# Two of the 24 modulation groups computed on TensorE between w_o and w_gate instead of on VectorE

## The chip, the cores and the metric

The kernel runs on one core of one Trainium2 chip. The metric is the device time of one execution in microseconds. Weights come from HBM by DMA, in chunks of one megabyte.

## What is computed

Two blocks in a row work on x, 256 positions by 2048 values, all in fp32. The first is a transformer block that is modulated by a second input c:

```python
mod = jax.nn.silu(c) @ w_ada[l] + b_ada[l]            # w_ada: 2048 x 12288
shift_a, scale_a, gate_a, shift_f, scale_f, gate_f = jnp.split(mod, ADA_CHUNKS, axis=-1)
h = rms_norm(x, g_attn_pre[l]) * (1.0 + scale_a[:, None]) + shift_a[:, None]
proj = h @ w_in[l]                                    # 2048 x 5456
...                                                   # two kinds of attention
mixed = jnp.concatenate([diff_out, dsa_out], axis=-1) @ w_o[l]
x = x + gate_a[:, None] * rms_norm(mixed, g_attn_post[l])
h = rms_norm(x, g_ffn_pre[l]) * (1.0 + scale_f[:, None]) + shift_f[:, None]
ff = (jax.nn.silu(h @ w_gate[l]) * (h @ w_up[l])) @ w_down[l]
x = x + gate_f[:, None] * rms_norm(ff, g_ffn_post[l])
```

The second block (latent attention, a convolution branch and their projections) uses no modulation and is not touched.

w_ada has 12288 columns, that is 24 groups of 512. Groups 0 to 3 are shift_a, 4 to 7 scale_a, 8 to 11 gate_a, 12 to 15 shift_f, 16 to 19 scale_f, 20 to 23 gate_f. Group 15 is the last quarter of shift_f, group 19 the last quarter of scale_f. Since x has 2048 columns, four groups of 512 make up one vector, and the fourth group serves the fourth quarter of the operand h alone.

## The kernel before

**Chunks and their ring.** `PLAN` (from `chunk_plan`, line 54) lists all 476 chunks of the program in one order. A chunk has 512 rows of a weight by up to 512 columns. SyncE loads them in that order into five buffers (`raw`, `NRAW` = 5): chunk c may be loaded when chunk c - 5 has been used (`load_chunk` in `sync_program`, the DMA at line 2440).

**A linear chunk** is two units. For each unit ScalarE copies 256 rows into a high half (`whi`, line 1033), VectorE subtracts it for the low half (`wlo`, line 1643), and TensorE makes three products out of them (lines 566 to 568, 12 matmuls of 512 columns a unit). `Walk.chunk` puts the splits of a unit into the queues of ScalarE and VectorE two units ahead (`AHEAD` = 2) of the place where its products stand:

```python
self.split_to(UNIT_AT[LIN[min(self.unit + AHEAD, len(LIN) - 1)]])
```

So while the last two units of w_o are worked off, the two units of the first w_gate chunk are split, and only then does the program go on to what follows w_o.

**A w_ada chunk** is used in one of two ways. Groups 8 to 23 are summed on VectorE (`ada_step`, line 1626: four passes a chunk of acc += raw * column, the first group of a row at line 1623, and one last sum at line 1635). Then TensorE turns the sum into columns of modT or into a row (`ada_take`, lines 501, 502 and 506), which runs as a side job in lane 1, and VectorE adds the bias (`mod`, line 1607). Groups 0 to 7 (`ADA_ON_PE`) are products of TensorE (`ada_products`, line 520): four matmuls a chunk with a stationary operand `cs32` of 32 columns, of which one holds silu(c) and 31 are zero. ScalarE copies the result out (`gather`), TensorE makes columns of it (`ada_columns`, line 531). These groups are needed first and are all done in the first quarter of w_in.

**What sets the order.** Every engine runs the same walk over the plan and emits its own part. Side jobs (attention in lanes 0 and 1, `soon` jobs in lane 2) advance one step per unit (`tick`). VectorE's w_ada chunks are dealt between the linear chunks by `more` in `chunk_plan`: 26 of them between the 24 later chunks of w_in (`W_IN_SHARE`), the remaining 16 between those of w_o (`W_O_SHARE` = 15), one after each chunk but the last.

**Between w_o and w_gate** stands a chain. For each output group `post_group` has ScalarE square it (line 1295) and VectorE multiply it by the gate (line 2073, `P<-bank,G` in the trace). After the last one VectorE makes the root's input (1688), ScalarE the root (1065), VectorE adds to x (1695, eight parts), ScalarE squares x (1302), VectorE makes `gs` (2110) and `diag` (1717), and TensorE turns the first quarter of x with it (`turn_quarter(0)`, line 582). Then follow shift and scale on VectorE (1744) and the high and low halves of the operand (1110, 1734), and w_gate begins.

## Time and profile before

| | |
|---|---|
| time, median of 3 runs | 2428.31 us (2427.94 to 2430.77) |
| the profiled execution | 2428.22 us, span 2426.9 us |
| TensorE matmuls busy | 2291.2 us, 94% |
| VectorE busy | 1399.5 us, 58% |
| ScalarE busy | 1062.3 us, 44% |
| mean DMA rate | 208 GB/s |

In the 40 slices of 60.7 us, TensorE is at nine tenths or more from the tenth slice on; before that it falls to seven and eight tenths in places. VectorE has 9 and 8 tenths in the fourth and fifth slice, then six, and four to five from the eleventh on. A share over the whole span says little here: the stages differ, and a saving counts only where TensorE waits.

### The profile page before, as it was taken

Reading aid. Unit: us, or ns where it says so; the run is one execution under the profiler, and the core shown is the slowest. Engines: PE = TensorE matmul, PEld = TensorE weight load, DVE = VectorE, ACT = ScalarE, POOL = GpSimd, SP = SyncE. Lnnn points to the kernel's source line nnn. Section 1 sums busy time; section 2 is a strip of 40 time slices with the busy share of each in tenths; the row PEclk is TensorE's granted clock in tenths of the full one; section 3 lists DMA queues with packets and bytes.
Section 4 is the critical chain, followed back from the end, with each engine's and each line's share of the span. In section 5 each row is a group of like instructions: output and inputs, shape, how many; then the busy total and the mean of one; then the engine's idle time right before and its main releaser. Section 6 shows DMA issues by size and latency. Waiting matters only on the chain.

```text
span 2426.9 us, 26309 instructions
## 1 busy us (share of the span) xinstructions
PE 2291.2 (94%) x10768; PEld 1861.1 (77%) x10768; DVE 1399.5 (58%) x1903; ACT 1062.3 (44%) x1469; POOL 0.7 (0%) x5
## 2 busy tenths in 40 slices
PE   4898989798999999999999999999999999999998
PEld 2676667676878888888887878788888888888886
DVE  1459898686666464454555555454544554554554
ACT  2333534444434444444444555555444444444443
POOL 0000000000000000000000000000000000000000
PEclk7999999899999999999999999999999999999999
DMA  7888678484776575556554644444555556556553
GB/s 296 333 314 306 216 262 285 153 306 166 247 273 243 192 259 191 191 191 191 191 189 143 210 157 154 153 152 152 185 196 192 188 184 197 183 186 194 187 190 139
DMA packets 255455, 505.69 MB, mean 208 GB/s; under 512 B 9077, under 2 KB 19662, under 8 KB 254182
## 3 DMA queue, kind: packets, MB, share of 16 engines
q1 hardware_dynamic: 255334, 504.00, 61.6%
q8 instruction: 85, 1.39, 0.2%
q14 instruction: 36, 0.29, 0.0%
HBM read 499.77 MB, written 4.19 MB: 208 GB/s over the span
## 4 chain that ended last, share of the span: by engine, by line
PE 82%; DVE 10%; ACT 3%; DMA 3%; issue 2%; SPq 0%; DVEq 0%; ACTq 0%
PE bank L566 26%; PE bank L568 25%; PE bank L567 25%; DVE wlo L1643 3%; DVE acc L1626 2%; PE bank L582 2%; DMA raw<-in_w_in_dram 2%; ACT whi L1033 1%; PE bank L650 1%; DMA raw<-in_w_ada_dram 1%; PE bank L520 1%; PE bank L590 1%; DVE x L1695 0%; ACT Ex_b L1162 0%; PE bank L673 0%
## 5 line engine op out<-in xcount | busy, mean ns | idle before, releaser
L1643 DVE TENSOR_TENSOR wlo<-raw,whi 128x1024 fp32r<-128x1024 f32 (+2 forms) x760 | 910.5, 1205 | 887.6 <-ACT whi L1033 887.1
L1033 ACT ACTIVATE whi<-raw 128x1024 fp32r<-128x1024 f32 (+2 forms) x760 | 790.1, 1044 | 1035.2 <-PE bank L568 949.1
L566 PE MATMUL bank<-whi,Ahi 128*128 128x512 f32 (+2 forms) x2304 | 912.5, 396 | 37.8 <-DVE wlo L1643 21.2
L567 PE MATMUL bank<-wlo,Ahi 128*128 128x512 f32 (+2 forms) x2304 | 897.0, 389 | 0.0
L568 PE MATMUL bank<-whi,Alo 128*128 128x512 f32 (+2 forms) x2304 | 896.6, 389 | 0.0
L566 PEld LDWEIGHTS bank<-whi,Ahi 128*128 128x128 f32 x2304 | 438.1, 190 | 141.1 <-DVE wlo L1643 31.3
L568 PEld LDWEIGHTS bank<-whi,Alo 128*128 128x128 f32 x2304 | 437.7, 190 | 90.3
L567 PEld LDWEIGHTS bank<-wlo,Ahi 128*128 128x128 f32 x2304 | 438.5, 190 | 83.2
L1626 DVE SCALAR_TENSOR_TENSOR acc<-raw,cs,acc 128x512 f32<-128x512 f32 x224 | 153.4, 746 | 0.0
L566 PE MATMUL bank<-whi,Fhi 128*128 128x512 f32 x352 | 137.7, 391 | 0.0
L568 PE MATMUL bank<-whi,Flo 128*128 128x512 f32 x352 | 137.0, 389 | 0.0
L567 PE MATMUL bank<-wlo,Fhi 128*128 128x512 f32 x352 | 137.0, 389 | 0.0
L566 PE MATMUL bank<-whi,Bhi 128*128 128x512 f32 x256 | 101.0, 395 | 0.0
L568 PE MATMUL bank<-whi,Blo 128*128 128x512 f32 x256 | 99.8, 390 | 0.0
L567 PE MATMUL bank<-wlo,Bhi 128*128 128x512 f32 x256 | 99.7, 390 | 0.0
L566 PEld LDWEIGHTS bank<-whi,Fhi 128*128 128x128 f32 x352 | 66.1, 188 | 14.3 <-issue 0.8
L568 PEld LDWEIGHTS bank<-whi,Flo 128*128 128x128 f32 x352 | 66.1, 188 | 14.0
L567 PEld LDWEIGHTS bank<-wlo,Fhi 128*128 128x128 f32 x352 | 66.1, 188 | 13.4
L520 PE MATMUL bank<-raw,cs 128*32 128x512 f32 x256 | 35.9, 681 | 21.3 <-DMA raw<-in_w_ada_dram 21.3
L568 PEld LDWEIGHTS bank<-whi,Blo 128*128 128x128 f32 x256 | 48.1, 188 | 10.2
L566 PEld LDWEIGHTS bank<-whi,Bhi 128*128 128x128 f32 x256 | 48.1, 188 | 9.9 <-issue 0.3
L567 PEld LDWEIGHTS bank<-wlo,Bhi 128*128 128x128 f32 x256 | 48.1, 188 | 9.6
(291 smaller groups left out, 1345.2 us busy)
## 6 DMA issues: line engine op xcount, KB each, us to landing
raw<-in_w_in_dram SPq DMA_DIRECT2D x156, 1024.0 KB, 5.0
raw<-in_w_ada_dram SPq DMA_DIRECT2D x96, 1024.0 KB, 5.3
raw<-in_w_gate_dram SPq DMA_DIRECT2D x44, 1024.0 KB, 5.1
raw<-in_w_up_dram SPq DMA_DIRECT2D x44, 1024.0 KB, 5.1
raw<-in_w_down_dram SPq DMA_DIRECT2D x44, 1024.0 KB, 5.0
raw<-in_w_o_dram SPq DMA_DIRECT2D x16, 1024.0 KB, 5.2
raw<-in_w_o_mla_dram SPq DMA_DIRECT2D x16, 1024.0 KB, 4.9
raw<-in_w_o_conv_dram SPq DMA_DIRECT2D x16, 1024.0 KB, 4.9
```

Of the source, the lines that this page charges most:

```text
L520: ins = pe.matmul(m.bank[b][32 * jj:32 * jj + 32, :], m.cs32[:, 4 * j + jj, :], m.raw[:, c % NRAW, jj, :], start=(j == 0), stop=(j == 3))
L566: pe.matmul(o, a_hi, w_hi, start=beg, stop=False)
L567: pe.matmul(o, a_hi, w_lo, start=False, stop=False)
L568: ins = pe.matmul(o, a_lo, w_hi, start=False, stop=fin)
L582: ins = pe.matmul(o, i, m.diag[:, tb, :], start=True, stop=True) if scaled else pe.transpose(o, i, m.ident)
L590: ins = pe.transpose(m.bank[b][:, tb * P:tb * P + P], src(tb), m.ident)
L650: pe.matmul(m.bank[ln.bank[mm]][:, PART[tb]], l, r, start=(i == 0), stop=False, skip_group_check=True)
L1033: act.activation(m.whi[:, i % NHL, :, 0:n], m.raw[:, c % NRAW, 2 * h:2 * h + 2, 0:n], ACT.Copy).then_inc(m.s_hi, 1)
L1626: ins = dve.scalar_tensor_tensor(out=o, in0=w, scalar=col, in1=o, op0=ALU.mult, op1=ALU.add)
L1643: dve.tensor_tensor(m.wlo[:, i % NHL, :, 0:n], m.raw[:, c % NRAW, 2 * h:2 * h + 2, 0:n], m.whi[:, i % NHL, :, 0:n].bitcast(F32), ALU.subtr ...
```

## The change

Groups 15 and 19 leave VectorE. Their eight chunks are taken out of the deal between w_in and w_o and stand in the plan after the last w_o chunk, numbers 132 to 139, right ahead of w_gate's first chunk, which is number 140 in both kernels. TensorE makes the products of all eight right behind the last w_o product, into banks 6 and 7. The gathering copies, the columns, the bias and the last quarter of the gains `gs` become side jobs inside the first w_gate linear. The stationary operand for them is a new tile `cs_gap`, filled by VectorE during w_o. The side jobs of the other groups use bank 4 instead of bank 6 from late in w_o on (`idle_bank`). VectorE's other chunks are dealt anew: 22 in w_in, 12 in w_o, none between the last four w_o chunks. A load that reuses the buffer of one of the new chunks waits for that chunk's product (`prod_at`).

```diff
-W_IN_SHARE = 26
-W_O_SHARE = 15
+W_IN_SHARE = 22
+W_O_SHARE = 12
-ADA_ON_PE = (4, 0, 5, 1, 6, 2, 7, 3)
+ADA_ON_PE = (4, 0, 5, 1, 6, 2, 7, 3, 15, 19)
...
-    rest = [("ada", g, j) for g in ADA_ON_PE for j in range(4)]
-    rest += [("ada", g, j) for g in range(8, 20) for j in range(4)]
+    rest = [("ada", g, j) for g in ADA_ON_PE[:8] for j in range(4)]
+    rest += [("ada", g, j) for g in range(8, 20) if g not in ADA_ON_PE for j in range(4)]
...
     assert not rest
+    plan += [("ada", g, j) for g in ADA_ON_PE[8:] for j in range(4)]
     rest = [("ada", g, j) for g in range(20, 24) for j in range(4)]
...
+        self.idle_bank = 6
...
+        self.cs_gap = sb("cs_gap", [P, KD, 32])
...
             _, g, j = PLAN[c]
-            b = 6 + ADA_ON_PE.index(g) % 2
+            idx = ADA_ON_PE.index(g)
+            b = 6 + idx % 2
+            need.wait_ge(m.s_cs, 1 if idx < 8 else 2)
+            cs = m.cs32 if idx < 8 else m.cs_gap
...
-                ins = pe.matmul(m.bank[b][32 * jj:32 * jj + 32, :], m.cs32[:, 4 * j + jj, :], m.raw[:, c % NRAW, jj, :],
+                ins = pe.matmul(m.bank[b][32 * jj:32 * jj + 32, :], cs[:, 4 * j + jj, :], m.raw[:, c % NRAW, jj, :],
                                 start=(j == 0), stop=(j == 3))
             ins.then_inc(m.s_prod if j < 3 else m.filled[b], 1)
+            m.prod_at[c] = (m.s_prod, 3 * idx + j + 1) if j < 3 else (m.filled[b], k.uses[b])
...
     mix_operand(12, (4, 5))
+    k.idle_bank = 4
...
+    def gap_columns():
+        ada_columns(8)
+        ada_columns(9)
+
+    def gate_side(j):
+
+        if j < 3:
+            k.soon(turn_quarter, 4 * j + 4)
+        if j == 0:
+            k.soon(gap_columns)
...
             linear("w_gate", 512 * cg, 512, m.A_op, shifted(8),
-                   before=lambda j: k.soon(turn_quarter, 4 * j + 4) if cg == 0 and j < 3 else None)
+                   before=gate_side if cg == 0 else None)
...
+    def gap_gather():
+        gather(4)
+        k.use(6), k.use(7)
...
     linear("w_o", 512, 512, ks=(4,), s=sets[1])
+    need.wait_ge(*rt_at[0])
+    v.up(dve.memset(m.cs_gap[:, :, :], 0.0))
+    settle()
+    dve.tensor_copy(m.cs_gap[:, :, 0], m.cs[:, :]).then_inc(m.s_cs, 1)
...
-    released(*(mod_at[g] for g in range(12, 20)))
-    v.up(dve.scalar_tensor_tensor(out=m.gs[:, :], in0=m.modT[:, 64:80], scalar=1.0, in1=m.cols[:, R_G2:R_G2 + 16],
-                                  op0=ALU.add, op1=ALU.mult))
+    def gains(q, n):
+
+        released(*(mod_at[g + i] for g in (12, 16) for i in range(q, q + n)))
+        ks = slice(4 * q, 4 * q + 4 * n)
+        v.up(dve.scalar_tensor_tensor(out=m.gs[:, ks], in0=m.modT[:, 64 + 4 * q:64 + 4 * q + 4 * n], scalar=1.0,
+                                      in1=m.cols[:, R_G2 + 4 * q:R_G2 + 4 * q + 4 * n], op0=ALU.add, op1=ALU.mult))
+
+    gains(0, 3)
...
+    def gap_mods():
+        for idx in (8, 9):
+            b = 6 + idx % 2
+            k.use(b)
+            mod(ADA_ON_PE[idx], b, k.use(b))
+        gains(3, 1)
+        settle()
...
-                idx, j = ADA_ON_PE.index(before[1]), before[2]
-                if j < 3:
-                    need.wait_ge(m.s_prod, 3 * idx + j + 1)
-                else:
-                    need.wait_ge(m.filled[6 + idx % 2], 2 * (idx // 2) + 1)
+                need.wait_ge(*m.prod_at[c - NRAW])
```

VectorE at the end of w_o in the kernel before. `P_76<-bank,G` is the first row of the chain between w_o and w_gate; the last two `wlo` rows ahead of it are the two units of w_gate's first chunk.

```order
L1626 SCALAR_TENSOR_TENSOR acc<-raw,cs,acc 128x512 [waits s_v] x2
L1635 TENSOR_TENSOR acc<-acc 128x512 [waits s_ada,s_v]
L1643 TENSOR_TENSOR wlo<-raw,whi 128x1024 [waits s_hi] x2
L1607 TENSOR_TENSOR modT<-bank,bT 128x4 [waits s_filled6]
L1643 TENSOR_TENSOR wlo<-raw,whi 128x1024 [waits s_hi] x2
L2073 TENSOR_TENSOR P_76<-bank,G 128x512 [waits s_psq] x2
L1688 TENSOR_REDUCE rstd<-ssq 128x2
```

The same place in the changed kernel (its line numbers are 30 or so higher).

```order
L1638 TENSOR_TENSOR modT<-bank,bT 128x4 [waits s_filled4]
L2104 TENSOR_TENSOR P_76<-bank,G 128x512 [waits s_psq] x2
L1674 TENSOR_TENSOR wlo<-raw,whi 128x1024 [waits s_hi] x8
L2104 TENSOR_TENSOR P_76<-bank,G 128x512 [waits s_psq] x2
L1719 TENSOR_REDUCE rstd<-ssq 128x2
```

VectorE's w_ada steps are gone from the last four w_o chunks; the two units of w_gate's first chunk still stand ahead of `P_76<-bank,G`.

SyncE's loads from the end of w_o to w_gate before:

```order
L2440 DMA raw<-in_w_ada_dram 128x4x512 [waits s_lo]
L2440 DMA raw<-in_w_o_dram 128x4x512 [waits s_ada]
L2440 DMA raw<-in_w_gate_dram 128x4x512 [waits s_lo]
L2440 DMA raw<-in_w_gate_dram 128x4x512 [waits s_ada]
L2440 DMA raw<-in_w_gate_dram 128x4x512 [waits s_lo]
L2440 DMA raw<-in_w_gate_dram 128x4x512 [waits s_ada]
L2440 DMA raw<-in_w_up_dram 128x4x512 [waits s_lo] x4
```

and in the changed kernel, where `s_prod` and `s_filled6` are raised by TensorE's products of the new chunks:

```order
L2491 DMA raw<-in_w_o_dram 128x4x512 [waits s_lo]
L2491 DMA raw<-in_w_ada_dram 128x4x512 [waits s_ada]
L2491 DMA raw<-in_w_ada_dram 128x4x512 [waits s_lo] x4
L2491 DMA raw<-in_w_ada_dram 128x4x512 [waits s_prod] x3
L2491 DMA raw<-in_w_gate_dram 128x4x512 [waits s_filled6]
L2491 DMA raw<-in_w_gate_dram 128x4x512 [waits s_prod] x3
L2491 DMA raw<-in_w_up_dram 128x4x512 [waits s_filled7]
```

The last three w_ada loads and the first four of w_gate wait for products of TensorE.

VectorE late in w_in, where the trace has a long run of w_ada steps, before:

```order
L1626 SCALAR_TENSOR_TENSOR acc<-raw,cs,acc 128x512 [waits s_v] x2
L1643 TENSOR_TENSOR wlo<-raw,whi 128x1024 [waits s_hi] x2
L1626 SCALAR_TENSOR_TENSOR acc<-raw,cs,acc 128x512 [waits s_v,s_raw1]
L1626 SCALAR_TENSOR_TENSOR acc<-raw,cs,acc 128x512 [waits s_ada]
L1626 SCALAR_TENSOR_TENSOR acc<-raw,cs,acc 128x512 [waits s_v] x2
L1626 SCALAR_TENSOR_TENSOR acc<-raw,cs,acc 128x512 [waits s_v,s_raw2]
L1626 SCALAR_TENSOR_TENSOR acc<-raw,cs,acc 128x512 [waits s_ada]
L1626 SCALAR_TENSOR_TENSOR acc<-raw,cs,acc 128x512 [waits s_v] x2
L1635 TENSOR_TENSOR acc<-acc 128x512 [waits s_ada,s_v]
L1643 TENSOR_TENSOR wlo<-raw,whi 128x1024 [waits s_hi]
L1607 TENSOR_TENSOR modT<-bank,bT 128x4 [waits s_filled6]
L1643 TENSOR_TENSOR wlo<-raw,whi 128x1024 [waits s_hi]
```

and now:

```order
L2061 SCALAR_TENSOR_TENSOR Ex_b<-Ex_b,sm_b 128x256 [waits s_v]
L1674 TENSOR_TENSOR wlo<-raw,whi 128x1024 [waits s_hi]
L1657 SCALAR_TENSOR_TENSOR acc<-raw,cs,acc 128x512 [waits s_raw3]
L1657 SCALAR_TENSOR_TENSOR acc<-raw,cs,acc 128x512 [waits s_ada]
L1657 SCALAR_TENSOR_TENSOR acc<-raw,cs,acc 128x512 [waits s_v] x2
L1666 TENSOR_TENSOR acc<-acc 128x512 [waits s_ada,s_v]
L1674 TENSOR_TENSOR wlo<-raw,whi 128x1024 [waits s_hi] x2
L1712 SCALAR_TENSOR_TENSOR Alo<-bank,gsub,Ahi 128x512 [waits s_oph,s_gsub]
```

One chunk's steps less stand ahead of the low halves there.

## Rows read from the trace of the kernel before

**Rows 1.** The page: busy time, share of the span and instructions of each engine.

```profile
PE 2291.2 (94%) x10768; PEld 1861.1 (77%) x10768; DVE 1399.5 (58%) x1903; ACT 1062.3 (44%) x1469; POOL 0.7 (0%) x5
```

**Rows 2.** Windows: busy time by engine, granted clock, DMA; the first row names the columns.

```profile
core 0: us, PE busy (x) PEld busy (x) DVE busy (x) ACT busy (x) POOL busy (x), PEclk, DMA share, GB/s
...
240.00:432.00 192.00, 166.76 (x829) 129.53 (x828) 167.85 (x335) 89.78 (x202) 0.00 (x0) 0.95 0.71 246
432.00:560.00 128.00, 111.16 (x533) 90.48 (x531) 97.15 (x154) 51.95 (x99) 0.00 (x0) 0.93 0.72 254
...
600.00:1200.00 600.00, 598.39 (x2652) 490.38 (x2651) 332.03 (x330) 249.61 (x260) 0.00 (x0) 1.00 0.65 218
```

**Rows 3.** Waits of TensorE, 280 to 560 us: total, times, longest.

```profile
PE bank L663 <- DVE Ex_b L2030: 16.6, 4, 8.8
...
PE bank L566 <- DVE wlo L1643: 3.7, 3, 2.8
```

**Rows 4.** The chain that ended last, 552 to 576 us: start, duration, what.

```profile
552.74 0.79 PE bank L506 x8
...
559.88 1.29 DVE P L2073 x2
...
569.43 3.78 PE bank L582 x16
...
574.04 0.47 PE bank L566
```

**Rows 5.** Timelines of TensorE, VectorE and ScalarE at the end of w_o.

```profile
558.73 0.39 PE L568 MATMUL bank<-whi,Alo 128*128 128x512 f32 x1
...
550.93 2.35 DVE L1643 TENSOR_TENSOR wlo<-raw,whi 128x1024 fp32r<-128x1024 f32 x2
...
557.53 1.23 DVE L1643 TENSOR_TENSOR wlo<-raw,whi 128x1024 fp32r<-128x1024 f32 x1 [2.38 <-ACT whi L1033]
...
559.15 0.60 ACT L1295 ACTIVATE P<-bank 128x512 f32<-128x512 f32 x1 [1.66 <-PE bank L568]
```

**Rows 6.** DMA issues, median us to landing last: 559 to 600, then 500 to 560.

```profile
raw<-in_w_up_dram SPq DMA_DIRECT2D x3, 1024.0 KB, 5.1
...
raw<-in_w_o_dram SPq DMA_DIRECT2D x7, 1024.0 KB, 7.1
```

**Rows 7.** Timeline of TensorE at the kernel's start, and a window there.

```profile
25.27 1.07 PE L520 MATMUL bank<-raw,cs 128*32 128x512 f32 x8 [0.95 <-DMA raw<-in_w_ada_dram]
34.78 1.93 PE L520 MATMUL bank<-raw,cs 128*32 128x512 f32 x8 [8.44 <-DMA raw<-in_w_ada_dram]
...
39.89 1.55 PE L520 MATMUL bank<-raw,cs 128*32 128x512 f32 x8 [0.62 <-DMA raw<-in_w_ada_dram]
...
34.78:42.00 7.22, 5.98 (x29) 1.23 (x30) 0.00 (x0) 0.32 (x1) 0.00 (x0) 0.57 1.06 406
```

**Rows 8.** Timelines in the first w_gate linear, ScalarE and TensorE.

```profile
581.84 1.99 ACT L1033 ACTIVATE whi<-raw 128x1024 fp32r<-128x1024 f32 x2
...
581.40 0.39 PE L566 MATMUL bank<-whi,Ahi 128*128 128x512 f32 x1
```

**Rows 9.** Timelines: three waits of TensorE, and VectorE ahead of two of them.

```profile
418.33 1.22 PE L650 MATMUL bank<-qT_b 64*128 64x256 f32 x4 [4.47 <-DVE modT L1607]
437.21 0.47 PE L663 MATMUL bank<-const,Ex_b 128*128 128x128 f32 x1 [2.78 <-DVE Ex_b L2030]
489.57 0.46 PE L673 MATMUL bank<-P,ET_a 128*128 128x128 f32 x2 [1.94 <-DVE ET_a L1912]
...
410.89 5.39 DVE L1626 SCALAR_TENSOR_TENSOR acc<-raw,cs,acc 128x512 f32<-128x512 f32 x8
...
428.77 4.07 DVE L1626 SCALAR_TENSOR_TENSOR acc<-raw,cs,acc 128x512 f32<-128x512 f32 x6
```

**Rows 10.** Two groups of TensorE instructions with first and last start, 600 on.

```profile
L501 PE MATMUL bank<-acc,const x8: 592/594/596, 667.9 to 897.0; 128*128 128x512 f32 x8
...
L582 PE MATMUL bank<-const,gt x8: 270/272/299, 674.5 to 678.0; 128*128 128x128 f32 x8
```

More of the change, by code:

```diff
@@ L382, in __init__ @@
         self.A_op = self.Ahi, self.Alo
+        self.prod_at = {}
         base = shelf.top
@@ L534, in idle @@
     def idle():
-        ada_take(k.take(), 6)
+        ada_take(k.take(), k.idle_bank)
         yield
@@ L629, in first_part @@
         return linear("w_in", *win_cols(cg), m.A_op, shifted(0), ks=(4 * q,))
-    need.wait_ge(m.s_cs, 1)
     ada_products(0)
@@ L1036, in idle @@
         k.take()
-        k.use(6)
+        k.use(k.idle_bank)
         yield
@@ L1321, in scalar_program @@
     mix_operand(12, (4, 5))
+    k.idle_bank = 4
     linear("w_o", 512, 512, ks=(4,), s=sets[1])
@@ L1344, in scalar_program, with gate_side @@
     F_at = [None]
+    def gap_gather():
+        gather(4)
+        k.use(6), k.use(7)
+    def gate_side(j):
+        if j < 3:
+            k.soon(shifted, m.tmpB, j + 1)
+        if j == 0:
+            k.soon(gap_gather)
     def ff_turn(kf):
@@ L1357, in scalar_program @@
         for cg in range(*third):
-            s = linear("w_gate", 512 * cg, 512,
-                       before=lambda j: k.soon(shifted, m.tmpB, j + 1) if cg == 0 and j < 3 else None)
+            s = linear("w_gate", 512 * cg, 512, before=gate_side if cg == 0 else None)
             k.finish_side()
@@ L1646, in idle @@
     def idle():
-        mod(k.groups[k.take()], 6, k.use(6))
+        mod(k.groups[k.take()], k.idle_bank, k.use(k.idle_bank))
         yield
@@ L2092, in vector_program @@
     mix_operand(12, (4, 5))
+    k.idle_bank = 4
     linear("w_o", 512, 512, ks=(4,), s=sets[1])
+    need.wait_ge(*rt_at[0])
+    v.up(dve.memset(m.cs_gap[:, :, :], 0.0))
+    settle()
+    dve.tensor_copy(m.cs_gap[:, :, 0], m.cs[:, :]).then_inc(m.s_cs, 1)
     y_at = []
@@ L2128, in ff_turn, with gate_side @@
         lo_pair(m.F_op, 4 * kf + 2, 5, [None])
+    def gap_mods():
[5 more added lines that the diff above has]
+        settle()
+    def gate_side(j):
+        if j < 3:
+            k.soon(ffn_operand, j + 1)
+        if j == 1:
+            k.soon(gap_mods)
     ffn_operand(0)
@@ L2133, in vector_program @@
         for cg in range(*third):
-            s = linear("w_gate", 512 * cg, 512,
-                       before=lambda j: k.soon(ffn_operand, j + 1) if cg == 0 and j < 3 else None)
+            s = linear("w_gate", 512 * cg, 512, before=gate_side if cg == 0 else None)
             gate_at = set_at(s)
@@ L2499, in build @@
         m = Machine(nc, A, out, ctx)
-        sync_program(m)
         tensor_program(m)
@@ L2504, in build @@
         gpsimd_program(m)
+        sync_program(m)
 def constants():
```

## The prediction

> **What bounds the kernel now.** I read the page first: TensorE is busy for 2291.2 of 2426.9 us [rows 1]. The windows by stage say where it is not [rows 2]. From 600 us on it is full (598.39 of 600), so nothing done for VectorE helps there. In 240 to 432 it is busy 166.76 of 192 us and VectorE 167.85; in 432 to 560, 111.16 of 128 and VectorE 97.15. These two stretches hold the attention steps, w_in and w_o, and VectorE's sums of w_ada, four passes a chunk. The view of waits names what TensorE lacked in 280 to 560, 40 us in all [rows 3]; the largest part, 16.6, belongs to one step of the attention chains (Ex_b), and only 3.7 to a weight half that came late (wlo). Then the chain through the pause [rows 4]: the last w_o product ends at 558.73 + 0.39 = 559.12 us, called E below. ScalarE and VectorE take the last group out of its banks (the latter from 559.88 on), norm it, square it, and at 569.43 TensorE turns x with diag; w_gate starts at 574.04. The pause is a chain of ScalarE and VectorE; TensorE stands idle for 10.3 us of it.
>
> **What stands just ahead of that chain** decides the case. VectorE runs its rows in order, and the low halves of the first w_gate chunk are split two units ahead: the second of the two is the row at 557.53, before the row at 559.88 [rows 4, 5]. The order shows the same in the changed kernel: of the eight wlo rows ahead of P, the last two are the halves of chunk 140, the first of w_gate. Before, that chunk had been in memory for long. Now eight w_ada chunks (132 to 139) are loaded ahead of it, through five buffers, and four of these loads, 137 to 140, may only be issued when TensorE's products of chunks 132 to 135 are done. Those stand in TensorE's queue behind the last w_o product. So chunk 140 is asked for after E, as the fourth of four loads, and the chain of the pause waits behind its splits.
>
> **The pause, step by step from E.** Chunks 132 to 136 are there at E: the last of them follows the split of the last w_o chunk, some 6 us before E (the pair of splits at 550.93 ended at 553.28, rows 5), and a lone megabyte lands in 5.1 us [rows 6]. A chunk's products took 1.07 us at best and 1.93 us at a granted clock of 0.57, the level of 1.2 GHz [rows 7]; after a stage at the full clock I take 1.07. So load 137 is issued at E + 1.2 and lands at E + 1.2 + 5.1 = 6.3. The next three were asked for by then (one product each 1.07 us) and follow at the rate of a full queue: in the start of the kernel the products of three chunks in a row begin from 34.78 to 39.89, 2.56 us apart, at 406 GB/s [rows 7]. Chunk 140 is there at 6.3 + 3 x 2.56 = E + 14.0. Its two splits take 1.06 us on ScalarE and then 2.35 us on VectorE (as the pair at 550.93, rows 5): E + 17.5. Only then comes the row that before began at E + 0.76. **The chain moves by 16.8 us**, and all that hangs on it. Bounds: 15 us if load 137 leaves right at E (5.1 + 7.7 + 1.06 + 2.35 - 0.76 = 15.5, and half a microsecond less for what I may have wrong in the handoffs), 19 us if loads land in 7.1 us as they do at 500 to 560 [rows 6]. Product 139 ends at about E + 11.5 + 1.9 = 13.4; that is cover, since the chain reaches diag only at 10.3 + 16.8 = E + 27.1. TensorE is idle before that turn again for over 10 us, so the turn's 3.78 us [rows 4] stay as they are. The loads of 141 to 144 finish inside the longer pause, so w_gate lacks nothing.
>
> The Trainium skill ("DMA: Bandwidth & Descriptors", section "Where 436 GB/s comes from") says that loads from HBM are held by the memory at about 358 GB/s a core. This trace shows 406 [rows 7]. By the page, 1.05 MB would take 2.93 us instead of 2.56 and the chain would move by 1.1 us more; the sum goes by the rows.
>
> **Added in w_gate.** ScalarE copies the products of groups 15 and 19 out (two copies), TensorE sums them into columns (eight small matmuls), VectorE adds the bias twice and makes the last four gains. The order puts the copies behind the first whi of the row at 581.84, and TensorE's columns ahead of its third unit, which began at 581.40 [rows 8]. That whi ends at 582.9, two copies of 0.6 (such a read of a bank took 0.60, rows 5) make 584.0; TensorE waits until then and needs 0.8 for the second group's columns (0.79, rows 4), 2.5 + 0.8. **+3.3 us**; bounds 1.6 (only the columns, twice 0.79) and 4.5 (a copy more of waiting). Groups 20 to 23 now use bank 4, which the turns of gt use too: TensorE's first row for such a group, at 667.9, lies 6.6 us ahead of the next turn, at 674.5, which waits for gt then anyway [rows 10], so I cost it at nothing; without that cover it would be one wait of about 1 us, four times.
>
> **Removed.** VectorE loses eight chunks of 2.7 us (eight passes took 5.39), 21.6 us, and two short sums at their ends that I leave out [rows 9]; TensorE loses twice 0.79 us of columns [rows 4]. What reaches the path is what TensorE waited for behind such a chunk: 4.47 us at 418.33, where VectorE had two chunks in a row (5.39), 2.78 at 437.21 after six passes (4.07), 1.94 at 489.57 after one chunk more, and 0.9 in the two short ones of the three waits for wlo (3.7 - 2.8): 10.1 us [rows 3, 9]. The order takes a chunk away before the first three; I take 8 of the 10.1. The other waits for Ex_b, 16.6 - 2.8 with one of 8.8 among them [rows 3], stand mostly behind the search for the top keys, where as many chunks stay. Against it: a side job more or less shifts lane b, and its last scores (qT_b) come one unit later, so that the last chain of attention has one unit (2.7 us, twelve products) less beside it; part of that is bought back since ScalarE's two softmaxes no longer meet. I charge 1.0. **-8.6 us** (8.0 + 1.6 - 1.0). Bounds: -23.2, if every microsecond of VectorE counted (21.6 + 1.6), and +3, if the shift costs a whole unit and nothing is won.
>
> The memset and copy of cs_gap on VectorE (under 1 us) fall where it loses a chunk; nothing.
>
> **Sum:** 16.8 + 3.3 - 8.6 = +11.5 us. The profiled run took 2428.22 us, 1.3 more than its span, and the median is 2428.31; so 2439.8 us.
>
> **Rivals.**
> *All of the relief counts.* VectorE is 87% busy in 240 to 432; if it sets the pace there from end to end, and the waits for Ex_b shrink too, the whole 23.2 us come off: 16.8 + 3.3 - 23.2 = -3.1, 2425 us, not slower. It decides from a relief of 20.1 us on. For it: that share, about TensorE's own. Against: TensorE's idle time there is what its named waits give, and those behind a chunk sum to 10.1 only.
> *The pause isn't held.* Should the splits of chunk 140 not stand ahead of the norm after all, the pause would grow only until product 139 is done, E + 13.4 against 10.3: 3.1 + 3.3 - 8.6 = -2.2, 2426 us. The order speaks against it.
> *The relief is eaten.* One unit less beside the last attention chain and new phases elsewhere: 16.8 + 3.3 + 3 = +23.1, 2451 us. For it: most of the 40 us are latencies between engines which no lighter queue shortens.
> *A slower stream.* If the loads land as they did under load at the end of w_o, 7.1 us after their issue instead of 5.1 [rows 6], chunk 140 comes 2 us later and the sum is 13.5: 2442 us.
>
> **How the numbers follow.** Forecast 0.60, all of the relief 0.10, not held 0.06, relief eaten 0.14, slower stream 0.10. A measurement tells 0.2% apart, 4.9 us: faster means under 2423.4, slower over 2433.2. Slower takes the forecast (all but a tail of relief above 15 us), the third and fourth rivals: 0.81. Faster, 0.05, is the far half of the first rival. The rest, 0.14, is the same. The range runs from 2430 to 2451: relief up to 18 us below, the third rival above.
>
> **What would show it.** VectorE's row P after the last w_o product: right if it starts 15 to 19 us after E (before 0.76) with the two wlo rows just ahead of it and "ACT whi" or the DMA of w_gate as what they waited for; wrong if it starts within 2 us. TensorE idle before the first turn in two pieces, between products for the DMA of w_ada, and some 13 us for diag. The first w_gate product about 31.7 us after E (before, at 574.04, 14.9). TensorE's waits at about 418 and 437 gone, and E itself 6 to 10 us earlier than 559.1; if E is later, the relief was eaten; if it is 20 us earlier, the first rival holds. A wait of 2 to 3 us before the columns in w_gate. Windows from 600 us on unchanged in length. The forecast is wrong above all if ScalarE or VectorE gets to the norm before w_gate's first chunk.

## The result and the profile after

| | before | changed |
|---|---|---|
| median of 4 runs | 2428.12 us (2427.86 to 2430.77) | 2451.52 us (2451.44 to 2452.88) |
| ratio | 1 | 1.0096, 95% interval 1.0084 to 1.0109 |
| span of the profiled execution | 2426.9 us | 2451.5 us |

The change costs 23.4 us. The forecast was 11.5 us, and the result lies half a microsecond beyond the end of the forecast's range. The page of the changed kernel, beside [rows 1], has TensorE 17 us busier and VectorE 21 us less busy:

```profile
PE 2308.1 (94%) x10832; PEld 1866.4 (76%) x10832; DVE 1378.8 (56%) x1872; ACT 1062.1 (43%) x1471; POOL 0.7 (0%) x5
```

Windows of the changed kernel, with the columns of [rows 2]:

```profile
240.00:557.00 317.00, 276.40 (x1339) 218.53 (x1339) 241.29 (x450) 135.33 (x285) 0.00 (x0) 0.94 0.66 226
557.00:588.00 31.00, 13.20 (x81) 5.22 (x80) 11.45 (x22) 9.73 (x25) 0.00 (x0) 0.63 0.80 304
588.00:604.00 16.00, 13.77 (x65) 11.40 (x66) 8.88 (x13) 5.70 (x8) 0.00 (x0) 0.82 0.16 45
640.00:1200.00 560.00, 558.09 (x2467) 456.77 (x2466) 312.58 (x314) 230.53 (x240) 0.00 (x0) 1.00 0.65 218
```

The pause is now 31 us, and the start of w_gate runs at a granted clock of 0.82. From 640 us on TensorE is as full as before; a loss of 2 us near 697, told below, is too small to show in so long a window. Four marks of TensorE's timeline split both spans without a remainder: E, the end of the last w_o product (559.12 us before, as in the prediction); the first w_gate product; the turn of the fourth quarter of x (the last thing particular to that linear); the end.

| us | before | changed | difference | forecast |
|---|---|---|---|---|
| E | 559.12 | 557.06 | -2.1 | -8.6 |
| E to the first w_gate product | 14.92 | 31.35 | +16.4 | +16.8 |
| first w_gate product to the fourth turn | 17.32 | 24.68 | +7.4 | +3.3 |
| fourth turn to the end | 1835.5 | 1838.4 | +2.9 | 0 |
| sum | | | +24.6 | +11.5 |

**The pause** went as forecast. The chain that ended last, in the changed kernel (start, duration, what; it answers to [rows 4]):

```profile
557.05 3.62 PE bank L529 x32
560.69 10.19 DMA raw<-in_w_gate_dram
570.89 1.07 ACT whi L1054
571.98 2.36 DVE wlo L1674 x2
574.35 1.20 DVE P L2104 x2
...
583.82 3.78 PE bank L592 x16
```

TensorE works off the products of the chunks that are there, the load of w_gate's first chunk lands at 570.89, E + 13.8, and only behind its splits comes VectorE's P row, 17.3 us behind E. TensorE's own rows in this stretch show the stream and the idle time ahead of the turn:

```profile
565.76 1.94 PE L529 MATMUL bank<-raw,cs_gap 128*32 128x512 f32 x8 [1.49 <-DMA raw<-in_w_ada_dram]
568.31 1.94 PE L529 MATMUL bank<-raw,cs_gap 128*32 128x512 f32 x8 [0.62 <-DMA raw<-in_w_ada_dram]
583.82 3.78 PE L592 MATMUL bank<-diag,x 128*128 128x128 f32 x16 [13.57 <-DVE diag L1748]
```

Loads whose products start 2.55 us apart are again more than 400 GB/s (the window of 561 to 571 gives 409), so the memory limit of 358 GB/s that the Trainium skill states ("DMA: Bandwidth & Descriptors", "Where 436 GB/s comes from") did not bind here.

**The relief** (the -8.6 us that were to come off ahead of E) did not come. Waits of TensorE in the changed kernel, 280 to 557 us (total, times, longest), beside [rows 3]:

```profile
PE bank L672 <- DVE Ex_b L2061: 12.0, 3, 7.3
PE bank L682 <- DVE ET_a L1943: 7.6, 3, 5.1
PE bank L576 <- DVE P L2076: 6.9, 1, 6.9
PE bank L576 <- DVE Alo L1710: 4.0, 1, 4.0
...
PE bank L659 <- DVE modT L1638: 0.6, 1, 0.6
```

In the kernel before, the same view had these for the same causes:

```profile
PE bank L663 <- DVE Ex_b L2030: 16.6, 4, 8.8
PE bank L566 <- DVE P L2045: 6.5, 1, 6.5
PE bank L650 <- DVE modT L1607: 4.5, 1, 4.5
...
PE bank L673 <- DVE ET_a L1912: 3.1, 3, 1.9
PE bank L566 <- DVE Alo L1679: 1.5, 1, 1.5
```

The waits that the forecast named are gone or short: 3.9 of 4.5 us for modT, the 2.8 for Ex_b at 437 (1.0 is left, for ScalarE), the 1.9 for ET_a at 489 [rows 9]. But a wait of 5.1 us for ET_a stands where 0.7 stood, the one for Alo is 2.5 us longer, and smaller ones are new. All waits of this view add up to 40.3 us now and to 39.9 before: VectorE has eight chunks less, and TensorE waits as long as it did. The 2.1 us by which E is earlier are about the size of what TensorE itself lost there, the columns of two groups (twice 0.79 us). VectorE's timeline ahead of the ET_a copy, changed kernel, with the row of TensorE that waited for it, shows why. TensorE began its transposes for that copy at 367.9 and has nothing left to do from 371.5 on:

```profile
369.64 2.73 DVE L1657 SCALAR_TENSOR_TENSOR acc<-raw,cs,acc 128x512 f32<-128x512 f32 x4
372.29 1.22 DVE L1674 TENSOR_TENSOR wlo<-raw,whi 128x1024 fp32r<-128x1024 f32 x1
...
374.35 0.29 DVE L1889 TENSOR_TENSOR P<-rt 128x128 f32<-128x128 f32 x1
...
374.76 1.22 DVE L1674 TENSOR_TENSOR wlo<-raw,whi 128x1024 fp32r<-128x1024 f32 x1
375.90 0.55 DVE L1943 COPY ET_a<-bank 128x384 f32<-128x384 f32 x1
...
376.59 0.77 PE L682 MATMUL bank<-P,ET_a 128*128 128x128 f32 x2 [5.14 <-DVE ET_a L1943]
```

and in the kernel before, where the transposes began at 369.5 and TensorE was busy until 374.0:

```profile
369.59 0.88 DVE L1623 TENSOR_SCALAR acc<-raw,cs 128x512 f32<-128x512 f32 x2
370.38 1.41 DVE L1626 SCALAR_TENSOR_TENSOR acc<-raw,cs,acc 128x512 f32<-128x512 f32 x2
371.71 2.35 DVE L1643 TENSOR_TENSOR wlo<-raw,whi 128x1024 fp32r<-128x1024 f32 x2
373.98 0.55 DVE L1912 COPY ET_a<-bank 128x384 f32<-128x384 f32 x1
...
374.68 0.46 PE L673 MATMUL bank<-P,ET_a 128*128 128x128 f32 x2 [0.68 <-DVE ET_a L1912]
```

A chunk stands ahead of the copy in both. Now six rows of the other lane's rotation (rt and P, 1.3 us) stand there too, so that the copy comes 1.9 us later, and TensorE is through with its own work 2.5 us earlier: together the 4.5 us by which the wait has grown. Dealing the chunks anew moved the lanes against each other.

**The first w_gate linear** has two stretches at the lower clock, 1.2 instead of 2.4 GHz (0.63 us a product instead of 0.39). Timeline of TensorE, changed kernel:

```profile
588.41 0.77 PE L576 MATMUL bank<-whi,Ahi 128*128 128x512 f32 x1 [0.81 <-issue]
...
591.53 0.63 PE L577 MATMUL bank<-wlo,Ahi 128*128 128x512 f32 x1
...
592.35 0.40 PE L576 MATMUL bank<-whi,Ahi 128*128 128x512 f32 x1
...
599.59 1.95 PE L541 MATMUL bank<-const,acc 128*128 128x1 f32 x16 [1.82 <-ACT acc L1076]
...
602.72 0.63 PE L578 MATMUL bank<-whi,Alo 128*128 128x512 f32 x1
...
605.70 2.07 PE L592 MATMUL bank<-diag,x 128*128 128x128 f32 x16
```

From the first product to the second turn it took 4.65 us, 2.84 before: +1.8. From there to the third turn 12.64 us against 7.24: 1.8 for the wait, 1.8 for the columns, 1.8 for the second stretch at 1.2 GHz. Of the last term of the table, 1.6 us are one more such stretch, after a wait of 1.91 us for gt at 697.06 (from there to the next turn of gt 4.8 us, against 3.2). Before, the wait was 1.61 us long [rows 10, at 674.5] and had full clock behind it. A wait of 0.5 us for a low half at 620.97 is new too; the last 0.5 us have no row of their own.

### The profile page after: what moved, and what is told of

Its sections match the earlier page's. It is cut to its first block, busy times and chain, and to the rows that moved or that the text cites. A ratio compares the mean times of both kernels' runs of the same rounds, so it can differ in the third digit from the quotient of the medians.

```text
span 2451.5 us, 26398 instructions
## 1 busy us (share of the span) xinstructions
PE 2308.1 (94%) x10832; PEld 1866.4 (76%) x10832; DVE 1378.8 (56%) x1872; ACT 1062.1 (43%) x1471; POOL 0.7 (0%) x5
## 4 chain that ended last, share of the span: by engine, by line
PE 82%; DVE 10%; ACT 4%; DMA 3%; issue 2%; SPq 0%; DVEq 0%; ACTq 0%
PE bank L576 25%; PE bank L578 25%; PE bank L577 25%; DVE wlo L1674 3%; DVE acc L1657 2%; DMA raw<-in_w_in_dram 2%; PE bank L592 2%; ACT whi L1054 1%; PE bank L659 1%; PE bank L529 1%; DMA raw<-in_w_ada_dram 1%; PE bank L600 0%; DVE x L1726 0%; DMA raw<-in_w_gate_dram 0%; ACT Ex_b L1183 0%
## 5 line engine op out<-in xcount | busy, mean ns | idle before, releaser
L1657 DVE SCALAR_TENSOR_TENSOR acc<-raw,cs,acc 128x512 f32<-128x512 f32 x196 | 134.4, 745 | 0.1
L578 PEld LDWEIGHTS bank<-whi,Blo 128*128 128x128 f32 x256 | 48.1, 188 | 10.3
```

Source lines behind the costliest of these rows:

```text
L578: ins = pe.matmul(o, a_lo, w_hi, start=False, stop=fin)
L1657: ins = dve.scalar_tensor_tensor(out=o, in0=w, scalar=col, in1=o, op0=ALU.mult, op1=ALU.add)
```

## The experiments

Theory: the pause is held by the splits of w_gate's first chunk; the relief was lost to where the deal puts VectorE's chunks among the lanes; the first linear lost twice to the clock. Each time below is a median, each ratio is to the kernel before on the same chip, with its interval. The marks are those of the table above; they come from the one execution of each kernel that was profiled, which can lie some microseconds beside its median. How far E moves by itself can be read off the six kernels that share the deal of 22 + 12 (changed, e1, e2, e3, e4, e8): it lies between 555.4 and 560.6.

| kernel | us | ratio | E | to w_gate | to 4th turn | rest |
|---|---|---|---|---|---|---|
| changed | 2451.5 | 1.0096 (1.0084 to 1.0109) | 557.1 | 31.4 | 24.7 | 1838.4 |
| e1, w_gate's chunk first | 2440.4 | 1.0044 (1.0027 to 1.0061) | 560.6 | 19.8 | 22.9 | 1837.5 |
| e2, columns later | 2446.8 | 1.0074 (1.0059 to 1.0089) | 557.0 | 31.3 | 21.0 | 1835.8 |
| e3, groups left out, 22 + 12 | 2430.3 | 1.0005 (0.9995 to 1.0014) | 556.0 | 14.9 | 19.0 | 1837.2 |
| e6, left out, 26 + 8 | 2422.7 | one execution | 549.8 | 14.9 | 19.6 | 1837.1 |
| e7, left out, 18 + 16 | 2417.8 | one execution | 545.0 | 15.1 | 19.4 | 1837.1 |
| e4, 26 idle products | 2453.1 | 1.0101 (1.0086 to 1.0116) | 558.0 | 34.4 | 22.9 | 1839.8 |
| e8, 14 idle products | 2450.4 | 1.0096 (1.0081 to 1.0112) | 555.4 | 30.2 | 22.8 | 1837.5 |
| e5, one group, 24 + 14 | 2430.9 | 1.0013 (1.0003 to 1.0022) | 551.4 | 16.8 | 25.9 | 1838.7 |
| e9, changed, 18 + 16 | 2447.8 | 1.0077 (1.0064 to 1.0091) | 551.1 | 31.3 | 24.9 | 1836.1 |
| e13, changed, 26 + 8 | 2441.0 | 1.0056 (1.0042 to 1.0069) | 550.3 | 31.4 | 24.5 | 1838.1 |
| e10, three mends, 18 + 16 | 2424.6 | 0.9985 (0.9976 to 0.9993) | 546.6 | 17.9 | 19.2 | 1837.0 |
| e16, three mends, 16 + 18 | 2429.9 | 1.0010 (1.0001 to 1.0019) | 554.6 | 18.6 | 19.2 | 1836.2 |
| e11, one group mended, 22 + 16 | 2440.9 | 1.0051 (1.0037 to 1.0065) | 562.4 | 19.5 | 20.2 | 1839.1 |
| before | 2428.1 | 1 | 559.1 | 14.9 | 17.3 | 1835.5 |
| e15, before, 24 + 18 | 2433.7 | 1.0033 (1.0021 to 1.0044) | 561.1 | 14.9 | 17.3 | 1835.6 |
| e12, before, 22 + 20 | 2442.8 | 1.0054 (1.0040 to 1.0067) | 568.5 | 14.9 | 17.3 | 1835.6 |
| e14, before, 30 + 12 | 2437.4 | 1.0035 (1.0022 to 1.0049) | 564.1 | 14.9 | 19.0 | 1837.5 |

### The pause: w_gate's first chunk loaded ahead of the eight

```diff
-    plan += [("ada", g, j) for g in ADA_ON_PE[8:] for j in range(4)]
+    gap = [("ada", g, j) for g in ADA_ON_PE[8:] for j in range(4)]
...
                     lin(w, 4 * q, 512 * cg, 512)
+                    plan += gap
+                    gap = []
...
     k.take_rest()
+    ada_products(PLAN.index(("ada", ADA_ON_PE[8], 0)))
     need.wait_ge(m.s_diag, 4)
```

> The changed kernel with one thing moved: the first chunk of w_gate is loaded before the eight chunks of groups 15 and 19, and TensorE still takes their products in the pause. Theory (the splits of that chunk, queued ahead of the norm's work on ScalarE and VectorE, hold the pause): the P row comes at E+1 instead of E+17.3 and the diagonals at E+10; but the eighth product, its load the fifth behind the last w_o product, ends about E+13.7, later than the diagonals, so that the first product of w_gate comes at E+18.5 instead of E+31.4. About 13 us less than the changed kernel, 2438.5. Rival 1 (the products themselves, or the loads' share of the memory, lengthen the pause): the first product of w_gate stays beyond E+28 and the time above 2448. Rival 2 (the second chunk of w_gate, now the last of the nine loads, is late instead): PE stalls inside the first linear for about 5 us and the time is about 2443.

Measured: the ratio falls by 0.52 points, some 12.6 us, and the way from E to w_gate from 31.4 to 19.8. VectorE's rows at the end of w_o, with P now 0.75 us behind E (560.62) as before the change:

```profile
559.03 1.23 DVE L1677 TENSOR_TENSOR wlo<-raw,whi 128x1024 fp32r<-128x1024 f32 x1 [1.44 <-ACT whi L1057]
561.37 1.29 DVE L2107 TENSOR_TENSOR P<-bank,G 128x512 f32<-128x512 f32 x2 [1.12 <-ACT P L1319]
```

and TensorE's:

```profile
575.82 3.30 PE L594 MATMUL bank<-diag,x 128*128 128x128 f32 x16
```

The splits were what held the pause; the products are not dear in themselves. What stays, 4.9 us, is the eighth load: the turn can start only behind its product, 15.2 us behind E, 1.5 later than I expected. E itself is 3.5 us later than in the changed kernel, with the same waits within 1 us each; the granted clock was 0.89 instead of 0.94 in 430 to 460 us and 0.79 instead of 0.87 in 460 to 500.

### The pause with one group

```diff
-ADA_ON_PE = (4, 0, 5, 1, 6, 2, 7, 3, 15, 19)
+ADA_ON_PE = (4, 0, 5, 1, 6, 2, 7, 3, 15)
...
         ada_columns(8)
-        ada_columns(9)
```

ScalarE's copy and VectorE's bias for group 19 go too, and the shares are 24 and 14.

> The changed kernel with group 15 alone on TensorE in the pause; group 19 is VectorE's again (24 of its chunks with w_in, 14 with w_o). Four chunks stand in the pause instead of eight, so that the first chunk of w_gate is the fifth load behind them and has landed when w_o ends. Theory (the pause is lengthened only by splits that wait for a late load): the P row comes at E+1, the diagonals at E+10, the first product of w_gate at E+15 as in the kernel before, where E is the end of the last w_o product; one column group instead of two takes 1 us less in the first linear. E near 558, in all 2434 to 2436. Rival (the products of chunks in the pause themselves cost, in proportion to their number): the first product of w_gate at E+23, the time about 2443.

Measured: 16.8 us from E to w_gate, and 1.0013. With four chunks in place of eight, w_gate's chunk is the fifth load, and the hold is nearly gone; P came 2.6 us behind E instead of 0.8, since its load landed only at 550.65. The rival, a cost in proportion to the products, is out: it had w_gate at E + 23. The time was better than I expected because E came at 551.4. The first linear took 25.9 us, not the 1 us less than in the changed kernel that I expected of a single column group: its two stretches at 1.2 GHz were 5.0 and 5.5 us long, against 4.1 and 3.2.

### The columns one chunk later

```diff
-        if j == 0:
+        if j == 1:
             k.soon(gap_columns)
```

> The changed kernel with TensorE's two column groups of 15 and 19 one chunk of w_gate later in its own order (behind the third quarter's turn instead of the second's); ScalarE and VectorE are as they were. Theory (TensorE reached them before ScalarE had gathered them, waited 1.82 us, and the half clock of 602.6 to 605.7 follows that wait and those small products): the wait goes, and the half-clock stretch with it, 3 to 3.5 us less, about 2448.3. Rival (the half clock comes from the small products alone, since 16 products of one column keep the engine little occupied): only the wait of 1.8 us goes and half clock comes after the columns all the same, about 2449.7. Rival 2 (VectorE now waits for the columns and the third operand is late): no gain, 2451.5 or more.

Measured: the first linear 21.0 instead of 24.7 us, the ratio 0.22 points lower (5.3 us, more than the 3 to 3.5 expected). The profiled span is 6.3 us shorter, but 2.6 of them lie behind the fourth turn, where the stretch at 1.2 GHz near gt did not come. TensorE:

```profile
600.25 1.95 PE L592 MATMUL bank<-diag,x 128*128 128x128 f32 x16
604.77 1.84 PE L541 MATMUL bank<-const,acc 128*128 128x1 f32 x16
609.33 1.95 PE L592 MATMUL bank<-diag,x 128*128 128x128 f32 x16
```

No wait, and full clock behind the columns (9.08 us from turn to turn, 7.24 + 1.84). The small products alone do not bring the half clock; in the changed kernel, and in e1, e4, e5, e8, e9 and e13 too, it followed the wait of 1.8 to 1.9 us with them behind it (in e13 the columns themselves already ran at it, 3.36 us instead of 1.95).

### Products of constants in the pause

```diff
     k.take_rest()
+    for r in range(26):
+        pe.matmul(m.bank[5][:, 0:384], m.ident, m.const[:, 0:384], start=True, stop=True)
     need.wait_ge(m.s_diag, 4)
```

> The changed kernel with 26 products of constants (384 columns, into a bank that nobody reads then) added on TensorE behind the eight chunks' products, in the idle 13.6 us of the pause; nothing else changes. Theory (the first products of w_gate ran at half the clock from 588.4 to 592.0 because the engine had been idle for 13.6 us, and the turn ahead of them too, 3.78 instead of 1.95): turn 1.8 us shorter, the first linear's start 1.8 us shorter, 3 to 3.6 us less, about 2448.2. Rival (the half clock there has another cause, such as the column groups' small products in the pause): no gain from the added products, 2451.5. Rival 2: they run at half clock throughout and end after the diagonals, which costs up to 3 us, 2454.

> The changed kernel with 14 products of constants in the pause instead of 26 (26 took 17.8 us at 0.68 us each, kept the full clock, but ended 4 us after the diagonals). Theory (the idle pause costs the clock): they end before the diagonals, the turn takes 1.95 us instead of 3.78 and the first quarter of w_gate's products 2.85 us instead of 4.65; 3 to 3.6 us less than the changed kernel, about 2448. Rival (what is won is given back later by a stretch at half clock elsewhere): the first quarter is shorter but the time stays within 1 us of 2451.5.

Measured: 26 ended 4 us too late (rival 2), but the turn took 1.95 us and the way to the second turn 2.85. With 14 they ended in time:

```profile
581.89 2.05 PE L592 MATMUL bank<-diag,x 128*128 128x128 f32 x16 [3.43 <-DVE diag L1747]
585.58 0.47 PE L576 MATMUL bank<-whi,Ahi 128*128 128x512 f32 x1 [1.63 <-issue]
588.42 1.95 PE L592 MATMUL bank<-diag,x 128*128 128x128 f32 x16
```

So the half clock at the start comes from the idle pause: 1.1 us less up to w_gate and 1.8 less in it. Yet the median is no better than that of the change by more than its uncertainty (1.0096 both times, to within 3 us for the change and 4 us for e8). The trace has the gain of 3 us, the timing neither shows nor excludes it.

### The relief: the groups left out, and three deals

```diff
-    plan += [("ada", g, j) for g in ADA_ON_PE[8:] for j in range(4)]
...
-            k.soon(gap_columns)
...
-            k.soon(gap_gather)
...
+    for g in (15, 19):
+        v.up(dve.memset(m.modT[:, 4 * g:4 * g + 4], 0.0))
...
-            mod(ADA_ON_PE[idx], b, k.use(b))
...
```

The products, copies and columns of groups 15 and 19 are left out, and their columns of modT are zeros, so that a quarter of the second operand is computed from other values. In the two further deals `W_IN_SHARE` and `W_O_SHARE` are 26 and 8, and 18 and 16; the second number is the count of w_o steps over which the rest is spread. With 16 steps a chunk stands behind each w_o chunk, the last one too; with 15, as before the change and in e9, e10 and e16, the last w_o chunk has none behind it.

> The changed kernel with groups 15 and 19 left out altogether (their loads, products, gather and columns; the eight columns of the modulation are zeros, so a quarter of the second operand is computed from other values). What stays of the change is the new deal of VectorE's chunks. Theory (from the trace of the changed kernel, whose last w_o product ends 2.1 us earlier than before): the last w_o product ends near 557, the pause is 14.9 us long, the first linear of w_gate runs as before, so about 2426.2 to 2426.5, at most 0.1% faster than the kernel before. Rival (the relief is the 8 us that the waits of before promised, and the loads of the eight chunks in the changed kernel ate it): the last product ends near 551 and the time is about 2420.

> As the run without groups 15 and 19 (their eight columns of the modulation are zeros), but the chunks of VectorE dealt 26 to w_in, as before the change, and 8 to w_o, instead of 22 and 12. Theory (the relief of 8 us of waits came, and the new deal of w_in's chunks made new waits of 5.1 us for ET_a and 2.5 us more for Alo by the places where a chunk stands ahead of a lane's copy): with the old deal in w_in the wait of 5.1 us for ET_a at about 376 is gone, the 4.5 us for modT at about 418 is back, and the waits of the w_o stretch shrink; the last w_o product ends at 552 to 556, instead of 556 to 557. Rival (the waits come with any deal of 34 chunks, being the lanes' own chains): the ET_a wait stays at 5 us and the end does not move by more than 1 us.

> As the run without groups 15 and 19, but dealt 18 to w_in and 16 to w_o (w_o as before the change, w_in relieved of all eight). Theory: the wait of 5.1 us for ET_a at 376 changes by over 1 us, since other operations now stand ahead of that copy, and the waits of the w_o stretch stay as in the kernel before (2.8, 1.9 and 0.9 us); the last product of w_o ends at 554 to 558. Rival (the lanes' own chains set the waits): within 1 us of the run dealt 22 and 12 both at 376 and at the end.

Measured: E at 556.0, 549.8 and 545.0 for the same 34 chunks, the last two from the only execution of their kernel. The pause is 14.9 again in the first two and 15.1 in the third. E came as forecast in e3, yet its median is no faster than the kernel before (2430.3, expected 2426.2 to 2426.5): 1.6 us went into a stretch at 1.2 GHz at the start of w_gate, 1.7 came behind the fourth turn, and the other executions were mostly longer than the profiled one. TensorE's wait for ET_a, in the runs with 26 and with 18 in w_in:

```profile
373.45 0.46 PE L681 MATMUL bank<-P,ET_a 128*128 128x128 f32 x2 [0.65 <-DVE ET_a L1938]
```

```profile
368.54 0.46 PE L681 MATMUL bank<-P,ET_a 128*128 128x128 f32 x2 [2.10 <-DVE ET_a L1938]
```

It is 5.15 us with 22. The rival (the lanes' own chains set these waits) falls. Both came earlier than I expected (552 to 556 with 26, 554 to 558 with 18). The 5 us between the two are no more than E moved under a single deal; that both are ahead of 22 is clear of it. With 26 the wait for modT at 417 is there again (4.45 us), with 18 it is not.

### Does the relief add to the whole change?

```diff
-W_IN_SHARE = 22
-W_O_SHARE = 12
+W_IN_SHARE = 18
+W_O_SHARE = 15
```

and 26 and 8 in the other run.

> The changed kernel, whole, with one number pair changed: VectorE's chunks dealt 18 to w_in and 16 to w_o (the latter as in the kernel before) instead of 22 and 12. Theory (the change lost most of its relief to the places of its deal): the last w_o product ends near 546 instead of 557, the pause and the first linear are as in the changed kernel, so that the time falls by 10 to 11 us to about 2441. Rival (the relief cannot be had together with the loads of the eight chunks, which were left out of the runs that showed it): the end stays near 557 and the time at 2450.

> The changed kernel, whole, dealt 26 to w_in (as before) and 8 to w_o. Theory (22 is a bad number, 26 is not, and the relief adds to the rest): the last w_o product ends near 550 instead of 557, as in the run without the groups, the pause is 31.3 us, the first linear 24.7; about 2445, 6 to 7 us less than the change. Rival (with the eight loads behind w_o only a part of the relief is left, since dealing 18 gave 4 us of 10): 2448 or more.

Measured: with 26, E at 550.3 and 10 us off the time, more than the 6 to 7 expected. With 18, E at 551.1 instead of 546 and only 4 to 5 us off. The order of TensorE's work up to E is that of e10 below, whose E was 546.6, and their waits agree but for one that is 1 us shorter in e9. What differs is the clock. Windows of 370 to 430 and 430 to 460 us, first e9, then e10 (the column ahead of the DMA share):

```profile
370.00:430.00 60.00, 54.72 (x267) 43.40 (x267) 47.04 (x89) 27.02 (x63) 0.00 (x0) 0.91 0.74 258
430.00:460.00 30.00, 26.06 (x152) 21.35 (x152) 19.77 (x41) 13.27 (x39) 0.00 (x0) 0.94 0.53 177
```

```profile
370.00:430.00 60.00, 52.85 (x273) 41.82 (x272) 48.09 (x90) 28.82 (x66) 0.00 (x0) 0.97 0.73 252
430.00:460.00 30.00, 23.07 (x141) 19.05 (x141) 18.46 (x42) 15.42 (x48) 0.00 (x0) 0.99 0.49 172
```

0.06 of 60 us and 0.05 of 30 are 5.1 us of full clock, against 4.5 us at E. By this estimate the clock accounts for the profiled execution; why the other executions of e9 were no faster, and what lowered the clock, is left open.

### Would another deal alone have done it?

```diff
-W_IN_SHARE = 26
+W_IN_SHARE = 22
```

and 24 in a second run, both on the kernel before; 30, with `W_O_SHARE` = 12, in a third.

> The kernel before with nothing changed but the deal of its 42 chunks: 22 with w_in and 20 with w_o instead of 26 and 16. Theory (the waits of the attention stage hang on where chunks stand among the lanes' jobs, so that the same work dealt otherwise gives another time): the end of w_o moves by over 2 us one way or the other, the times lie outside 2426 to 2430. Rival (only the number of VectorE's chunks counts): within 1.5 us of 2428.

> The kernel before, its 42 chunks dealt 24 to w_in and 18 to w_o. Dealt 22 and 20 it took 2442.8, by a wait of 5.2 us for ET_a at 378, of 1.4 to 1.8 us for three splits in w_o, and clock. Theory: between the two, the ET_a wait 2.9 us as in the one-group run dealt 24; w_o ends near 559 to 563, the time 2428 to 2433. Rival (the number dealt to w_in beyond 22 does not matter): within 1 us of 2428.

> The kernel before, its 42 chunks dealt 30 to w_in and 12 to w_o. No eight chunks leave VectorE. Theory (places count for more than number): the end of w_o moves by over 2 us from 559, either way; nothing says which. Rival (26 and 16 is the best that 42 chunks allow, so that a gain needs fewer of them): 2430 or more. If it comes under 2424.6 the gain of the mended change is had by dealing alone.

Measured: 22 in w_in costs 13 us by its ratio, 9.5 us in the profiled execution, in a kernel in which nothing has left VectorE:

```profile
377.56 0.77 PE L673 MATMUL bank<-P,ET_a 128*128 128x128 f32 x2 [5.15 <-DVE ET_a L1912]
```

The same wait as in the changed kernel, one of 3.6 us for ScalarE's Ex_b at 436.79 that the kernel before does not have, and with 20 chunks in w_o three new ones of 1.35 to 1.75 us for splits. 24 and 30 were slower than 26 too. So the relief needs both: fewer chunks (no deal of 42 that ran had E under 559) and a deal that fits.

### The three mends together

e10 is the change with 18 and 16, w_gate's chunk first and the columns later; e16 has 16 and 18; e11 has one group, its columns later, ten idle products and 22 and 16.

> The changed kernel with three things mended together: dealt 18 and 16, the first chunk of w_gate loaded ahead of the eight, the columns one chunk later. Theory (the three are separate terms and add): last w_o product 546, first w_gate product 20 us behind it at 566 (before: 574.0), the first linear 3 us longer than before for the columns and no half clock; about 2422, 5 to 6 us less than the kernel before. Rival (where the pause ends earlier, the loads of w_gate's second and third chunk, behind nine others, are late): waits for loads of 3 to 6 us in the first linear, about 2427.

> The change with its three mends, dealt 16 to w_in and 18 to w_o instead of 18 and 16 (2424.6). Theory (places): the end of w_o moves by over 1 us from 546.6 either way; w_o's stretch, with two chunks more, brings split waits like those of the kernel before dealt 22 and 20, so rather later, 2425 to 2429. Rival (fewer in w_in is better throughout): 2420 to 2423.

> One group (15) in the pause, VectorE's chunks dealt 22 to w_in and 16 to w_o, the column group one chunk later, and ten products of constants behind the group's products in the idle 8.6 us of the pause. Theory: last w_o product between 546 and 551, the diagonals 12.2 us behind it (group 15's stream left w_gate's first split 2 us late), the turn at full clock, the first w_gate product at 562 to 567, the first linear 1 us longer than before; 2417 to 2422, the fastest of all. Rival (the deal of 38 chunks with 22 in w_in brings new waits, as 22 did with 34): the end stays beyond 555 and the time at 2427 or more.

Measured: e10 is faster than the kernel before, by 0.15% (0.07 to 0.24), 3.6 us; its profiled span is 6.2 us shorter. TensorE there:

```profile
559.86 1.06 PE L531 MATMUL bank<-raw,cs_gap 128*32 128x512 f32 x8 [1.56 <-DMA raw<-in_w_ada_dram]
560.85 2.05 PE L594 MATMUL bank<-diag,x 128*128 128x128 f32 x16
564.53 0.47 PE L578 MATMUL bank<-whi,Ahi 128*128 128x512 f32 x1 [1.63 <-issue]
```

The products run right up to the turn, which has full clock. The three terms add, to the 6.2 us of the span: E 12.5 us earlier, 3.0 more in the pause, 1.8 more in the first linear, 1.5 later on. The median gained less, and came at 2424.6 instead of the 2422 expected. The rival (late loads of w_gate's next chunks) did not come. Two chunks more in w_o (e16) move E by 8 us to 554.6, more than I expected, and the gain is gone. e11 met its rival: with 22 in w_in the wait for ET_a is 5.12 us, E at 562.4. Its idle products ended 4.7 us ahead of the turn, and the turn had half the clock again (3.78 us); in e8 they ended 3.4 us ahead of it, and it had full clock.

## Why the prediction was half right

- **What bounds the kernel, and the chain of the pause: right.** P ran 17.3 us behind E (forecast 17.5), w_gate's chunk landed at E + 13.8 (14.0), the loads were 2.55 us apart (2.56), the turn came at E + 26.8 (27.1), the first w_gate product at E + 31.4 (31.7). The term was +16.8 and measured +16.4. (The steps as I wrote them add up to 17.4 and +16.6, not to 17.5 and +16.8.) e1 shows the cause: with the chunk ahead of the eight, P is back at E + 0.75.
- **Added in w_gate, +3.3: mis-sized, +7.4.** The wait and columns made 3.6 us. What I left out is the clock, 1.8 us behind the wait and 1.8 at the start. I reasoned only that the turn ahead of w_gate would stay at half clock, as it was before, and not that the products behind it could too: before, TensorE had full clock from 574.04 on, here from about 592. e2 and e8 show both.
- **Removed, -8.6: the step that failed.** It took the waits that stood behind a chunk of VectorE and removed them one by one. Those did go, some 8 us. But it treated the rest of the deal as fixed, with 1.0 us for the shift of a lane, where about as much arose anew: 7 us by the waits for ET_a and Alo alone. TensorE's waits up to E came to 40.3 us, against 39.9 before, and E moved by 2.1 us in place of 8.6. The size of -8.6 was not out of reach: with the old number in w_in the change has E 8.8 us earlier (e13), with 18, 12.5 (e10). It was the deal of 22 that lost it: the same wait for ET_a is 5.14 us here, 5.15 in e12, where nothing left VectorE, and 0.65 with 26 in e6. And in the order of the changed kernel the rows ahead of the ET_a copy could have been read.
- **Windows behind 600 us unchanged: nearly.** 2.9 us were lost there, which I had put at nothing, 1.6 of them to half clock behind the wait for gt at 697. That wait grew by 0.3 us. I had costed bank 4's new users at nothing, and nothing ties it to them: over all kernels that use bank 4 it is 1.6 to 3.0 us, over the four deals of the kernel before, which do not, 1.55 to 1.96. What brings the half clock there is left open.
- **The rivals.** The time fell on that of the third, relief eaten, 2451, and that is in part a coincidence. Its mechanism was half there: a new phase of the lanes gave back what the chunks had left, but E was still 2.1 us earlier where the rival had it 3 us later, and stretches at 1.2 GHz made up the rest. None of the others came.

## What to carry to other kernels

When work is taken off an engine that runs its queue in order, what is left of it must be dealt again, and the deal can be worth more than the work: the same 34 chunks put the end of the stage at 545 to 556 us, and the same 42 at 559 to 569, where kernels with a single deal differed by up to 5 us from one profile to the next. Read, in the new order, what stands ahead of each row that another engine waits for, and try two or three deals before judging the move itself. When chunks are put into a stream of loads, look at which split is issued ahead of the chain behind it: one chunk moved ahead of eight was worth 12 us.

## What the runs showed of the hardware

- A wait of 1.8 us of TensorE followed by eight or sixteen matmul rows of one column was followed by a stretch of 2.8 to 5.5 us at 1.2 GHz in all seven kernels that had it (changed, e1, e4, e5, e8, e9, e13); the same small products without the wait were not (sixteen in e2, e10 and e16, eight in e11).
- At the first turn of gt all kernels wait for VectorE. In the four where the wait was 1.91 us or longer (changed 1.91, e14 1.96, e13 2.03, e5 3.00) a stretch at 1.2 GHz of some 1.6 us cost followed; in the fourteen where it was 1.55 to 1.86 us none did. No run changed this wait by itself, so it is not shown to be the cause.
- Ahead of the first turn of x, 3.4 us of idle time behind fourteen products of constants left it at full clock (e8, the turn took 2.05 us), 4.7 us behind ten did not (e11, 3.78 us).
- Behind the idle pause w_gate began at full clock in the kernel before, e12, e13 and e15, and at half clock in the changed kernel, e2, e3, e5, e6, e7, e9, e11 and e14, though before, e3 and e14 have the same 10.3 us of idle time and the same slow turn ahead of it. What decides is left open; the first products up to the second turn take 4.4 to 5.1 us with it and 2.8 without, so that differences of 2 to 4 us between single executions of this kernel say little.
